# Seven block products in place of eight in all six halves of three feed-forwards

## Chip, cores and metric

The kernel runs on one core of a Trainium2 chip. The metric is the device time of one execution in microseconds, as the median of three runs.

## What is computed

A small diffusion transformer in fp32: width 1024, 256 latent and 256 context tokens, first a block of two layers (a gated linear attention mixer, then a state-space mixer), then a second block of two layers (attention with convolution, then sliding-window and differential attention with a mixture of experts). Each layer takes six modulation vectors from a product of one condition vector with a 1024 x 6144 matrix. The change touches three feed-forwards:

```python
def sq_relu_mlp(h, w1, w2):                  # block 1, layers 0 and 1: w1 1024x4096, w2 4096x1024
    return jnp.square(jax.nn.relu(h @ w1)) @ w2
# block 2, layer 0: w1, w3 1024x2816, w2 2816x1024
# y = (silu(u @ w1) * (u @ w3)) @ w2
# after each: hl = layer_norm(ALPHA * hl + gate * y), or in block 2 hl + gate * y and rms norm ahead of the next mixer
# modulation: m = split(silu(c) @ ada_w[i] + ada_b[i], 6)
```

Layer 0 of block 1 and layer 0 of block 2 work on 512 tokens, layer 1 of block 1 on the 256 latent ones. (The context of the second block is another input, loaded into hT after layer 1's hidden part.)

## The kernel before, in words

Everything is feature major: hT (the residual stream) and uT (the modulated input) hold 8 tiles of 128 features by 512 tokens. A list of stages is built near L2699; each engine runs its own part of each stage in order (`run`, L2736). A stage that isn't `joined` starts with a barrier among TensorE, ScalarE and VectorE (`stage`, L2747): each drains, counts, and waits for the other two. GpSimd runs only stages that are `pooled`.

**Banks.** TensorE's products go round six of the eight PSUM banks (`Banks`, L118). `empty` waits for the bank's last reader, `full` for the product, `freed` for its reader. **Weights.** SyncE streams blocks of up to 2 MB into four slots in a fixed order (`Weights`, L151; L2806); a slot is loaded again when the last product that used it is done.

**Hidden layer, squared ReLU** (`HiddenRelu2`, L932). Eight blocks of 512 columns. Each of 32 hidden tiles is eight 128x128 products with all T tokens (`feature_major`, L821, matmul at L828); the first four tiles run k by k as uT's tiles arrive (`first_features`, L835, L846). ScalarE takes the ReLU from PSUM, VectorE squares it into the arena.

**Down projection** (`Residual`, L858). Eight output tiles, each 32 (or 22) products with all T tokens, one after the other; VectorE adds gate times the product from PSUM to hT (L907), ScalarE squares the new tile (L682), VectorE adds tile and square to two sums (L695, L698). Behind the last tile come the mean and variance (`Norm`, L643), and the next stage's first products wait for the normed and modulated tiles. A barrier stands ahead of this stage.

**Gated hidden layer** (`HiddenSwiglu`, L2179). Its first two tiles are plain; the others go in pairs as seven products (`Seven`, L2078), 128 weight columns by 256 tokens by four k tiles. ScalarE copies the first product, VectorE makes eight additions, GpSimd makes four 512-column sums of weight blocks (L2122 to L2124 and L2130), three of them in a two-deep scratch or in place.

**Guests** (`AdaGuest`, L493). The modulation vectors of later layers are made beside the feed-forwards, 256 columns at a time: ScalarE's queue loads 1 MB into one of two rooms, VectorE adds eight k tiles, each times its condition entry (L576 the first, L573 the other seven, twice that where latent and context are both wanted: a two-sided guest), and TensorE turns the result with two or four short products (L528). A guest has a place among the stage's products; its sums are made at place - 2, the load of the one after the next is issued at place - 1. Before: 24 guests in layer 0's hidden stage (8 two-sided), 24 in its down projection (all two-sided), none in layer 1, 24 in the gated hidden stage (8 two-sided), none in the last down projection.

## Time and profile before

| | us |
|---|---|
| median of 3 runs | 3199.26 (3198.19 to 3200.58) |
| span of the profiled execution | 3197.3 |
| TensorE matmul busy | 3044.7 (95%) |
| VectorE, ScalarE, GpSimd busy | 1338.9, 544.4, 107.2 |
| HBM read | 428.32 MB, 134 GB/s |

The page has a table of busy time by engine, the span in 40 slices, the DMA queues, the chain of work that ended last, and the costliest groups of instructions. The profiled execution is given by its span alone. Matmuls are pipelined, so the mean time of one record is longer than its share of a steady stream: for the price of one, busy time is divided by the count. A 128x128 fp32 weight block against up to 512 columns is two records.

### The profile page before, as it was taken

What the parts mean: (1) busy time and instruction counts of PE and PEld (TensorE: products, weight loads), DVE (VectorE), ACT (ScalarE), POOL (GpSimd) and SP (SyncE); (2) the same over time, 40 slices, a digit from 0 to 9 for tenths busy, and PEclk for the clock granted to TensorE, in tenths of its full rate; (3) what the DMA queues carried; (4) which work ended last, traced back from release to release, by engine and by line L of the source; (5) the groups of instructions that cost most, each with busy time, mean ns of one, the idle gap of its engine ahead of it and who ended that gap; (6) DMA issues with size and microseconds to landing.
All of it is one profiled execution on the core that took longest, in us unless ns stands there. A gap on an engine that the chain in (4) does not pass through costs nothing.

```text
span 3197.3 us, 33171 instructions
## 1 busy us (share of the span) xinstructions
PE 3044.7 (95%) x13248; PEld 2060.0 (64%) x13248; DVE 1338.9 (42%) x3117; ACT 544.4 (17%) x1149; POOL 107.2 (3%) x84
## 2 busy tenths in 40 slices
PE   7999889999999999899999998999999979999999
PEld 2448444444456666788844555888446656999998
DVE  3566465467647777321031327875013342000011
ACT  0215110000033434121021221000012331000000
POOL 0000000000000000000000002343000000000000
PEclk9999999999999999999999999999999988999999
DMA  7550145566322222345521103544222011887785
GB/s 259 171 171 27 53 161 183 156 189 180 115 66 60 79 80 75 109 146 136 154 84 68 53 27 129 174 164 129 76 92 80 27 53 67 289 301 265 267 290 194
DMA packets 395321, 431.58 MB, mean 135 GB/s; under 512 B 15449, under 2 KB 307960, under 8 KB 395034
## 3 DMA queue, kind: packets, MB, share of 16 engines
q1 hardware_dynamic: 294320, 329.77, 31.8%
q10 hardware_dynamic: 100842, 99.62, 9.7%
q8 instruction: 108, 1.77, 0.2%
q14 instruction: 51, 0.42, 0.0%
HBM read 428.32 MB, written 1.05 MB: 134 GB/s over the span
## 4 chain that ended last, share of the span: by engine, by line
PE 90%; DVE 4%; ACT 2%; issue 1%; DMA 0%; DVEq 0%; ACTq 0%
PE bank L828 45%; PE bank L2569 10%; PE bank L2150 7%; PE bank L846 6%; PE bank L2583 4%; PE bank L854 4%; PE bank L528 2%; PE bank L1942 1%; DVE arena L573 1%; PE bank L1935 1%; PE bank L2551 1%; PE bank L2595 1%; PE bank L1539 1%; PE bank L1559 1%; PE bank L1927 1%
## 5 line engine op out<-in xcount | busy, mean ns | idle before, releaser
L828 PE MATMUL bank<-uT,slot 128*128 128x512 f32 (+2 forms) x2208 | 784.9, 512 | 0.0
L828 PE MATMUL bank<-arena,slot 128*128 128x512 f32 (+1 forms) x2016 | 694.0, 506 | 12.9 <-DVEq L2749 10.6
L828 PEld LDWEIGHTS bank<-uT,slot 128*128 128x128 f32 (+1 forms) x2208 | 416.3, 191 | 320.5 <-issue 296.8
L828 PEld LDWEIGHTS bank<-arena,slot 128*128 128x128 f32 x2016 | 386.3, 193 | 299.2 <-issue 275.1
L573 DVE SCALAR_TENSOR_TENSOR arena<-arena,sT 128x256 f32<-128x256 f32 x784 | 365.6, 520 | 7.4
L2569 PE MATMUL bank<-arena,slot 128*128 128x128 f32 x2816 | 316.2, 275 | 3.1 <-issue 2.5
L2569 PEld LDWEIGHTS bank<-arena,slot 128*128 128x128 f32 x2816 | 315.2, 192 | 5.8 <-issue 5.8
L846 PE MATMUL bank<-uT,slot 128*128 128x512 f32 (+1 forms) x448 | 180.4, 568 | 24.7 <-ACT uT L595 12.5
L2654 DVE TENSOR_TENSOR arena<-bank,halves 128x256 f32<-128x256 f32 (+1 forms) x48 | 19.3, 402 | 432.1 <-ACT halves L2615 432.1
L907 DVE SCALAR_TENSOR_TENSOR hT<-bank,mod,hT 128x256 f32<-128x256 f32 (+1 forms) x88 | 36.7, 455 | 370.6 <-PE bank L828 370.6
L846 PEld LDWEIGHTS bank<-uT,slot 128*128 128x128 f32 x448 | 93.1, 209 | 111.7 <-issue 106.4
L2583 PE MATMUL bank<-slot,arena 128*128 128x256 f32 x704 | 153.3, 379 | 1.0 <-DVEq L145 1.0
L2150 PE MATMUL bank<-uT,slot 128*128 128x256 f32 x640 | 148.0, 379 | 0.8 <-DVE arena L2176 0.8
L2583 PEld LDWEIGHTS bank<-slot,arena 128*128 128x128 f32 x704 | 133.7, 190 | 19.3 <-issue 1.2
L2150 PEld LDWEIGHTS bank<-uT,slot 128*128 128x128 f32 x640 | 121.4, 190 | 18.2 <-issue 1.9
L854 PE MATMUL bank<-slot,uT 128*128 128x512 f32 (+2 forms) x352 | 127.3, 515 | 5.7 <-issue 5.7
L682 ACT ACTIVATE halves<-hT 128x512 f32<-128x512 f32 (+1 forms) x49 | 26.4, 538 | 576.5 <-DVE hT L907 531.1
L982 DVE TENSOR_TENSOR arena<-halves 128x512 f32<-128x512 f32 (+1 forms) x64 | 35.7, 558 | 203.8 <-ACT halves L972 203.6
L854 PEld LDWEIGHTS bank<-slot,uT 128*128 128x128 f32 x352 | 62.7, 203 | 66.7 <-issue 66.3
L2122 POOL TENSOR_TENSOR arena<-slot 128x512 f32<-128x512 f32 x20 | 28.2, 1411 | 1868.1 <-DVEq L2749 1868.1
L573 DVE SCALAR_TENSOR_TENSOR rstd<-arena,sT,rstd 128x256 f32<-128x256 f32 x224 | 90.0, 477 | 0.0
L1663 DVE SCALAR_TENSOR_TENSOR arena<-arena,vectors 128x512 f32<-128x512 f32 (+1 forms) x128 | 87.7, 685 | 4.5
(360 smaller groups left out, 2727.0 us busy)
## 6 DMA issues: line engine op xcount, KB each, us to landing
arena<-in_ada_w ACTq DMA_DIRECT2D x88, 1024.0 KB, 5.3
slot<-in_ffn_w SPq DMA_DIRECT2D x42, 2048.0 KB, 9.0
slot<-in_moe_w SPq DMA_DIRECT2D x32, 2048.0 KB, 10.0
slot<-in_moe_w SPq DMA_DIRECT2D x32, 1408.0 KB, 8.9
slot<-in_moe_w SPq DMA_DIRECT2D x16, 1536.0 KB, 9.1
slot<-in_ssd_w_in SPq DMA_DIRECT2D x32, 512.0 KB, 6.8
slot<-in_gla_w_in SPq DMA_DIRECT2D x6, 2048.0 KB, 10.3
slot<-in_ev_w_in SPq DMA_DIRECT2D x6, 2048.0 KB, 7.9
```

The lines of the kernel that those rows point to most:

```text
L528: ins = pe.matmul(ada_cols_bank[:, o:o + 1], acc[:, s, j * P:j * P + P], one[:, 0:1], start=True, stop=True)
L573: ins = dve.scalar_tensor_tensor(out=acc[:, s, :], in0=w[:, k, :], scalar=c, in1=acc[:, s, :], op0=ALU.mult, op1=ALU.add)
L828: ins = pe.matmul(bank[0:m, 0:t1 - t0], w[:, k, c0:c0 + m], x[:, k, t0:t1], start=(k == 0), stop=(k == kt - 1))
L846: ins = pe.matmul(bank[0:m, 0:t], w[:, k, c0:c0 + m], uT[:, k, 0:t], start=(k == 0), stop=(k == KD - 1))
L854: ins = pe.matmul(bank[:, 0:c1 - c0], x[:, k, t * P:t * P + P], w[:, k, c0:c1], start=(k == 0), stop=(k == kt - 1))
L907: return dve.scalar_tensor_tensor(out=h, in0=y, scalar=self.m[:, 8 * self.q + k, s:s + 1], in1=h, op0=ALU.mult, op1=ALU.add)
L982: dve.tensor_tensor(self.hid[:, i, :], r, r, ALU.mult).then_inc(*S("free_a").given())
L1539: ins = pe.matmul(bank[:, h * P:h * P + P], s_dab[k % 2][:, h, :], tri[z], start=True, stop=True)
L1663: ins = dve.scalar_tensor_tensor(out=acc, in0=s_raw[:, j, 0:n, tap:tap + LAT], scalar=vc("conv_w", 32 * tap + f), in1=acc, op0=ALU.mult, o ...
L2150: ins = pe.matmul(bank[:, 0:LAT], a[:, k, :], x[:, k, :], start=(k == 0), stop=(k == self.H - 1))
L2569: ins = pe.matmul(bank[:, o:o + P], w[:, k, (f - c) * P:(f - c) * P + P], m_x[:, k, e * P:e * P + P], start=(k == 0), stop=(k == KD - 1))
L2583: ins = pe.matmul(bank[:, 0:256], hid[:, k, :], w[:, k, :], start=(k == 0), stop=(k == NFE - 1))
```

## The change

The six halves all go by a form of Winograd's scheme with seven products in place of eight: a unit of weights (k tiles in two halves, columns in two halves) times the input (k tiles in two halves, tokens in two halves).

- **Units.** Hidden: 8 k tiles x 512 columns, products of 4 k tiles x 2 column tiles x T/2 tokens. Down: the k tiles are cut in two chunks (16 + 16, or 12 + 10), a unit is one chunk x 256 columns, products of 8 (or 6, 5) k tiles x 1 column tile x T/2 tokens. Order 11, 12, S1, 22, S2, S4, S3; a hidden stage starts with 11 and 12 of its first two units.
- **Weight sums.** GpSimd makes four sums a unit, of a quarter of the unit each (1024 columns, or 768 and 640 in the last down projection), in the slot itself; the second waits for product 11, the third for 12, the fourth for 22.
- **Token differences.** VectorE makes four at the start of each hidden stage and of each chunk of a down projection: the first in place, the others in the arena; a column count of 4 (or 8, 6, 5) x T/2.
- **Evacuation.** ScalarE copies product 11; VectorE makes six operations from PSUM, two of them onto both token halves. The hidden non-linearity is made on whole units by ScalarE. In a down projection the result goes to `halves`, and two (or four) additions put it onto hT at the end of each unit, for each chunk; the norm's squares and sums go along with chunk 1, two tiles a unit.
- **Barriers.** Down is `joined`; signals (hid_done, tiles_done, token_sums, weight_sums, ctx_in) take the barrier's place.
- **Guests** are spread anew: layer 0 hidden 16 (8 two-sided), down 16 (8 two-sided), layer 1 hidden 6 and down 6 (all two-sided), gated hidden 24 (12 two-sided), last down 4 (one-sided). Sums come 4 or 7 products ahead of the guest's place, in two or four parts.
- Six tables of constants are no longer resident, but loaded at the start of OddProject.

```diff
-        class HiddenRelu2(Stage):
+        class Seven:
+            ORDER = ("11", "12", "S1", "22", "S2", "S4", "S3")
+            TOKENS = {"S1": 1, "22": 2, "S3": 1}
...
+            def product(self, pe, bank, w, name, fresh, streamed=None):
+                if name in ("S1", "S2", "S4", "S3"):
+                    pe.wait_ge(*S("weight_sums").taken("pe"))
+                if fresh and name in self.TOKENS:
+                    pe.wait_ge(*S("token_sums").taken("pe", self.TOKENS[name]))
...
+                a = {"11": a11, "12": a12, "S1": a21, "22": a22, "S2": a11, "S4": a12, "S3": a22}[name]
+                x, n, us = self.right[name], self.n, range(a.shape[2] // P)
+                for u in us:
+                    for k in range(self.h):
+                        if streamed and u == 0:
+                            streamed()
+                        ins = pe.matmul(bank[:, u * n:u * n + n], a[:, k, u * P:u * P + P], x[:, k, :], start=(k == 0),
+                                        stop=(k == self.h - 1))
+                ins.then_inc(full_sem, 1)
...
+            def pool(pool, B, w, at):
+                made = S("weight_sums")
+                a11, a12, a21, a22 = Seven.blocks(w)
+                pool.tensor_tensor(a21, a21, a22, ALU.add).then_inc(*made.given())
+                B.full(pool, at("11"))
+                pool.wait_ge(made.sem, made.made)
+                pool.tensor_tensor(a11, a21, a11, ALU.subtract).then_inc(*made.given())
+                B.full(pool, at("12"))
+                pool.wait_ge(made.sem, made.made)
+                pool.tensor_tensor(a12, a12, a11, ALU.subtract).then_inc(*made.given())
+                B.full(pool, at("22"))
+                pool.tensor_tensor(a22, a22, a11, ALU.subtract).then_inc(*made.given())
...
+        class Down(Stage):
+            joined = True
+            pooled = True
+            NU = KD // 2
...
+                cut = 2 * -(-kt // 4)
+                self.chunks = [(0, cut), (cut, kt)]
...
+            def act(self, act, B, ch):
+                if self.guest:
+                    B.full(act, -1)
+                    self.guest.begin(act)
+                self.norm.act_begin(act)
+                for i, (c, u, name) in enumerate(self.order):
+                    if name == "11":
+                        if c + u:
+                            act.wait_ge(S("tiles_done").sem, self.before + c * self.NU + u)
+                        if c and u:
+                            self.norm.act_tile(act, B, 2 * u - 2)
+                            self.norm.act_tile(act, B, 2 * u - 1)
+                        Seven.act(act, B, Tiles(self.out), i)
...
+            def dve(self, dve, B, ch):
+                dve.wait_ge(*self.src.made(self.chunks[0][1]))
+                self.sevens[0].token_sum(dve, 1)
+                B.full(dve, -1)
+                for step in (2, 4, 3):
+                    self.sevens[0].token_sum(dve, step)
+                if self.src.guest:
+                    self.src.guest.dve(dve, ch)
...
+                    if name == "S3":
+                        B.freed(dve, self.index[c, u, "12"])
+                        B.freed(dve, self.index[c, u, "S4"])
+                        B.freed(dve, i)
+                        for j in range(2):
+                            f = 2 * u + j
+                            ins = self.add(dve, j, f, 0, slice(0, LAT))
+                            if self.T == TOK:
+                                ins = self.add(dve, j, f, 1, slice(LAT, TOK))
+                        ins.then_inc(*S("tiles_done").given())
+                    if self.guest:
+                        self.guest.sums(dve, ch, i)
...
-        hid = HiddenRelu2(I["ffn_w1"][0], TOK, AdaGuest(0, 1, all_six, spread, (0, 1)))
-        stages += [hid, Residual(I["ffn_w2"][0], hid.hid, 32, M[0], 5, TOK, False,
-                                 AdaGuest(1, 0, all_six, spread, all_six), Norm(8, M[1], 0, TOK, True))]
+        hid = HiddenRelu2(I["ffn_w1"][0], TOK, AdaGuest(ada01[0:4], spread(8, 52, 16), hidden_guest, 4, 2))
+        stages += [hid, Down(I["ffn_w2"][0], hid, M[0], 5, Norm(8, M[1], 0, TOK, True),
+                             AdaGuest(ada01[4:6] + ada10[0:2], spread(5, 50, 16), down_guest, 4, 2))]
...
+        hid = HiddenRelu2(I["ffn_w1"][1], LAT, AdaGuest(ada10[2:5], spread(14, 52, 6), late_guest, 7, 4, stop=6), ctx=True)
+        stages += [hid, Down(I["ffn_w2"][1], hid, M[1], 5, Norm(24, M[2], 0, LAT, False, True),
+                             AdaGuest(ada10[2:5], spread(8, 48, 6), late_guest, 7, 4, skip=6))]
...
+                           AdaGuest(ada10[5:6] + ada11[0:5], spread(8, 78, 24), late_guest, 4, 2))
+        stages += [hid, Down(I["ffn_w2_2"][0], hid, M[2], 5, Norm(None, M[3], 0, TOK, False),
+                             AdaGuest(ada11[5:6], spread(8, 48, 4), down_guest, 4, 2))]
```

## Rows read from the trace of the kernel before

**Rows 1.** The page's table: busy time, share of span, instructions by engine.
```profile
PE 3044.7 (95%) x13248; PEld 2060.0 (64%) x13248; DVE 1338.9 (42%) x3117; ACT 544.4 (17%) x1149; POOL 107.2 (3%) x84
```
**Rows 2.** Busy time by stretch (length, engines, granted clock, DMA share, GB/s): feed-forward halves.
```profile
393.26:644.13 250.87, 240.95 (x640) 114.74 (x640) 137.67 (x306) 28.46 (x46) 0.00 (x0) 0.96 0.50 159
647.56:892.20 244.64, 244.64 (x706) 120.08 (x707) 162.34 (x414) 4.41 (x7) 0.00 (x0) 0.99 0.53 155
892.20:900.12 7.92, 3.16 (x8) 1.16 (x7) 5.84 (x11) 2.86 (x5) 0.00 (x0) 0.95 0.25 66
1371.20:1484.89 113.69, 113.69 (x514) 99.58 (x515) 16.75 (x42) 19.99 (x46) 0.00 (x0) 0.97 0.47 144
1488.55:1599.30 110.75, 110.75 (x513) 97.52 (x514) 11.46 (x26) 5.47 (x15) 0.00 (x0) 1.00 0.51 145
1931.25:2227.80 296.55, 289.21 (x1312) 242.03 (x1312) 221.59 (x424) 25.53 (x41) 103.21 (x77) 0.98 0.45 146
2231.84:2385.87 154.03, 154.03 (x353) 68.16 (x354) 10.29 (x20) 4.41 (x7) 0.00 (x0) 0.98 0.30 85
```
**Rows 3.** Groups by form (busy us, mean ns, then idle before): matmuls by columns.
```profile
L828 PE MATMUL bank<-arena,slot 128*128 128x512 f32 x1120 | 496.6, 603 | 10.6 <-DVEq L2749 8.3 <-DVE arena L1321 2.3
...
L2569 PE MATMUL bank<-arena,slot 128*128 128x128 f32 x2816 | 316.2, 275 | 3.1 <-issue 2.5 <-DMA slot<-in_moe_w 0.5
```
**Rows 4.** The chain that ended last, in order of time (start, length, piece).
```profile
454.77 6.97 PE bank L828 x16
462.53 6.97 PE bank L828 x16
...
499.99 6.97 PE bank L828 x16
507.30 6.97 PE bank L828 x16
...
2068.27 12.20 PE bank L2150 x56
```
**Rows 5.** Timeline (start, length, engine, line; idle before in brackets), first hidden stage.
```profile
427.98 1.66 PE L528 MATMUL bank<-const,arena 128*128 128x1 f32 x8 [4.91 <-DVE arena L573]
...
434.65 1.87 PE L528 MATMUL bank<-const,arena 128*128 128x1 f32 x8 [5.00 <-DVE arena L573]
...
436.38 8.98 PE L828 MATMUL bank<-uT,slot 128*128 128x512 f32 x14
```
**Rows 6.** Timeline: first products of the three down projections.
```profile
647.56 12.63 PE L828 MATMUL bank<-arena,slot 128*128 128x512 f32 x22 [3.43 <-DVEq L2749]
...
1488.55 11.68 PE L828 MATMUL bank<-arena,slot 128*128 128x256 f32 x53 [1.64 <-DVEq L2749]
...
2231.84 4.60 PE L828 MATMUL bank<-arena,slot 128*128 128x512 f32 x5 [3.98 <-DVEq L2749]
```
**Rows 7.** Timeline, gated hidden stage: guest additions without and beside GpSimd's sums.
```profile
1985.77 3.25 DVE L573 SCALAR_TENSOR_TENSOR arena<-arena,sT 128x256 f32<-128x256 f32 x8
...
1993.16 7.27 DVE L573 SCALAR_TENSOR_TENSOR arena<-arena,sT 128x256 f32<-128x256 f32 x8
1993.36 1.41 POOL L2130 TENSOR_TENSOR slot<-slot,arena 128x512 f32<-128x512 f32 x1 [8.52 <-PE bank L2150]
...
1997.64 1.32 POOL L2124 TENSOR_TENSOR arena<-slot 128x512 f32<-128x512 f32 x1
...
2000.49 1.86 PE L528 MATMUL bank<-const,arena 128*128 128x1 f32 x8 [6.52 <-DVE arena L573]
```
**Rows 8.** Groups by form: a weight sum, a VectorE product, a residual addition.
```profile
L907 DVE SCALAR_TENSOR_TENSOR hT<-bank,mod,hT 128x256 f32<-128x256 f32 x72 | 32.5, 480 | 330.2 <-PE bank L828 330.2
...
L2123 POOL TENSOR_TENSOR slot<-slot 128x512 f32<-128x512 f32 x20 | 26.5, 1323 | 1.6
...
L2288 DVE TENSOR_TENSOR arena<-arena,halves 128x1024 f32<-128x1024 f32 x10 | 13.9, 1387 | 0.8
```
**Rows 9.** Groups by form within the gated hidden stage: all guest additions.
```profile
L573 DVE SCALAR_TENSOR_TENSOR arena<-arena,sT 128x256 f32<-128x256 f32 x224 | 131.3, 620 | 3.4
```

More of the change, by code:

```diff
@@ L522, in pe @@
                     return
+                if n == 0 and self.order:
+                    pe.wait_ge(S("guest_read").sem, self.order)
                 acc = self.room[1][n % 2]
@@ L887, in act @@
                 for k in range(KD):
-                    if self.guest:
-                        self.guest.loads(act, range(4 * k, 4 * k + 4))
                     if self.norm:
@@ L901, in dve @@
                 for k in range(KD):
-                    if self.guest:
-                        self.guest.sums(dve, ch, range(4 * k, 4 * k + 4))
                     bank = B.full(dve, k)
```

628 lines of the change are left out of this document (339 added, 289 removed).

## Prediction

> **What bounds the kernel now.** I read the page's table of busy time first: TensorE is busy 95% of the span and GpSimd 3% [rows 1]. So a microsecond of TensorE work is worth nearly a microsecond wherever it stands, and the question is what the fewer products wake up. Next a table by stretch, one line for each of the six feed-forward halves [rows 2]: H0 and D0 (hidden layer and down projection, 512 tokens), H1 and D1 (256 tokens), HS and D2 (gated hidden layer, 22-tile down projection, 512 tokens). The reader is to see that TensorE is busy in all of each stretch but some 10 us in H0 and 7 us in HS, that VectorE has half or more of H0, D0 and HS, and little in H1 and D1, which have no guest. Then the prices by shape [rows 3]: each fp32 product counts as two records, so a 128x128 block against 512 columns costs 2 x 0.443 us. Then the chain [rows 4]: a group of seven against 256 columns is 56 records in 12.20 us, 0.218 each; against 128 columns the experts' 2816 records take 316.2 us, 0.1123 each. So 256 and 128 columns cost the same per column within 4%: the narrow products of the 256-token halves aren't bound by weight loads.
>
> **1. TensorE's own work.** A unit of H0, H1 or HS (8 x 512 weights) is seven products of two tiles by four blocks: 7 x 8 x 2 = 112 records. A unit of D0 or D1 (a 16 x 256 block) has 7 x 8 x 2 = 112 too.
> H0: 8 units x 112 x 0.218 = 195.2 us. Guests cost TensorE 0.79 us with two sides (pitch 7.76 against 6.97) and 0.34 with one (7.31) [rows 4]; it now has 8 of each: 9.0. Before, the first hidden tiles took four products for each tile of uT that arrived; now two narrow ones. A tile takes VectorE two operations of 512 columns and one of 256, about 0.6 + 0.6 + 0.4 us by the nearest rows [rows 8], and TensorE has done its share of it in 0.44 x 2, so it starves: first four products end at about 18.9 us instead of 14.0, +4.9. Sum 209.1 against 250.9 [rows 2]: **-41.8**. That takes in that the guest at place 2 made TensorE wait 4.91 and 5.00 us, after which 14 records took 8.98 us instead of 6.1 [rows 5]; now the first guest is at place 8 of 56.
> D0: 195.2 + 9.0 = 204.3 against 244.6: **-40.3**.
> H1: 896 x 0.1123 = 100.6, six two-sided guests 4.7, slow start 2.6 (I take the same as its start now costs): 107.9 against 113.7: **-5.8**. D1: 105.3 against 110.8: **-5.4**. A quarter of the gain per column is lost to the narrow width and half the rest to guests that move in.
> HS: ten full units and two of half: 1232 x 0.218 = 268.5, guests 12 x 0.79 + 12 x 0.34 = 13.6, start 2.6: 284.7 against 296.6: **-11.9** (it had seven products in all but two tiles; its waits of 6.5 and 0.8 us go too). D2: 4 x 7 x 11 x 2 = 616 records, 134.2, guests 1.4: 135.6 against 154.0: **-18.4**.
> Sum -123.6 us. If every price were the widest row's, only the last digit moves; what can eat it stands in the next parts.
>
> **2. Barriers.** Between a hidden layer and its down projection TensorE stood 3.43 us (D0), 3.98 us (D2) and 1.64 behind the context's transposes (D1) [rows 6]: -9.0. In their place TensorE's fourth product (the one with factor a22) waits for VectorE: last half's evacuation, then token differences 1, 2 and 4, each 2048 columns in D0 (about 2.5 us, twice the 1.39 of a 1024-column operation [rows 8]), 1024 in D1. VectorE is done near 10.5 us after the hidden layer's last product, plus one GpSimd sum that holds it; TensorE is there at 10.5. I put 3.3 + 2 + 3 = +8.3 us. Price from both sides: 0 if no sum falls in, 15 if each difference meets one.
>
> **3. Tails.** A Down's last product must be added (1024 columns), then four residual additions of 0.45 us [rows 8], then two squares and additions of the norm that lay beside TensorE's last tile before, and the mean's four matmul pairs start only then. Before, the 7.9 us behind D0 [rows 2] held only the last tile's two additions. I add 5 (D0), 2.7 (D1), 3.5 (D2, no mean) = +11.2. From both sides: 6 and 20.
> So far -113.1 us.
>
> **4. GpSimd's sums.** A full unit needs four in-place sums of 1024 columns. No row shows one on GpSimd. The nearest is 512 columns: 1.32 us [rows 8]. Bounds: 1.32 (no growth) and 2.65 (proportional); I take 2.45, since VectorE's price grows a little less than in proportion. The Trainium skill's GPSIMD Engine Reference (3.1 Elementwise) gives 4497 ns for 2048 fp32 elements, which with its dispatch share makes an estimate of 2.3 to 2.4 us: it would change no term. Four sums are about 10 us in a unit of 24.4 us (512 tokens) and in one of 12.6 (256 tokens). The in-place order allows it: after product 11, sums 2, 3 and 4 must be there before S3 starts, 9 us later at 256 tokens; they take 7.6. Cover is there while a sum is under about 2.9 us in H1 and D1 and 5.5 elsewhere.
>
> **5. What the sums do to VectorE.** This is the term that decides. In HS eight guest additions (two SBUF inputs) take 3.25 us without GpSimd and 7.27 us beside four of its sums, and TensorE then waits 6.52 us [rows 7]: a sum that meets them costs VectorE its length less one addition, 1.0 us. Over all of HS the 224 additions take 131.3 us instead of 224 x 0.406 = 91 [rows 9]: 40 us for 77 sums, 0.52 of a hit each, and with the first operation of each guest, which that row doesn't hold, I take 0.65; where VectorE is behind all the time, 0.85. Evacuations read one input from PSUM, and I count them as free. With sums of 2.45 us the price is about 2.1 us, and there are 176 sums in the five halves with many guests: up to 370 us on VectorE. What of it reaches TensorE depends on VectorE's slack there. The Trainium skill's SBUF — State Buffer (Who interferes with whom) says the shared pair is an exclusive lock held for the whole instruction, by a VectorE instruction with two SBUF inputs or by a GpSimd one. By that rule the trace agrees: the 7.27 us row; without the lock the sum would end at parts 1 to 3.
> Per unit, VectorE against TensorE, at a share of 0.65 to 0.85 hits per sum. H0: evacuation 4 x 0.65 + 2 x 1.3 = 5.2, two-sided guests 2.4 x 6.3 (sixteen operations at 0.4) = 15.1, hits 5.5 to 7.1: 25.8 to 27.4 against 26.3 us: +2. HS the same with the gate's product: +3. D0: chunk 1 adds residuals 2.1 and norm 3.2 to 14.7 of guests and 5.2: 30.7 to 32.3 against 26.2, over 3.3 units, with a lag of 8 us brought from the token differences at the end of chunk 0, less what six banks cover (about 14 us): +14. H1: evacuation 3.1, guests 5.5, hits 5.5 to 7.1: 14.1 to 15.7 against 13.3 over six units: +8. D1: 9.5 (chunk 0) and 11.5 (chunk 1) plus hits, 15.0 to 18.6 against 13.3, and 8 us late at its start: +22. D2: +1. Sum **+50 us**, from 6 (banks absorb all but D1's late start) to 119 (below).
>
> **6. Edits at nothing.** Guests' DMA is the same 88 MB spread over more stages, weights come in rows twice as long in the down projections, and the DMA share in these stretches is 0.30 to 0.53 [rows 2]; late constants load behind OddProject's first products; ScalarE has 4 to 28 us of each stretch. If a load were late it would show as TensorE waiting for a slot, some us each.
>
> **Sum.** -123.6 - 9.0 + 8.3 + 11.2 + 50 = -63 us. Against the profiled execution's span of 3197.3 us this is 3134; the median of the runs, 3199.3, is 2.0 above the span, so **3136 us**. A measurement tells about 0.2%, 6.4 us, from no change.
>
> **Rivals.**
> A, the banks absorb the blocking. Six banks let VectorE fall some five products behind, 17 us at 512 tokens, and the guests are asked for four to seven places after their sums. For it: HS already has this blocking and TensorE lost only 7.3 us to it. Against: the sums are twice as long and five halves have them, and D1 has half the time per product. Part 5 is then 6 to 20: 3092 to 3106. Chance 0.22.
> B, every sum stops VectorE for its length (slower). VectorE's lists with all hits at 2.1 us: H0 197 against TensorE's 209 (nothing), D0 238 against 204 (+34), H1 132 against 108 (+24), D1 158 against 105 (+53), HS 293 against 285 (+8): +119, all in stages where VectorE can't keep step, 3205 us, slower by 6. It decides from a share of 1 at 2.1 us a sum, and each 0.1 us more on a sum adds some 12 us. For it: around 1993 us all four sums hit [rows 7]. Against: over HS as a whole the share was 0.52 to 0.65 [rows 9], since VectorE idles between products. Chance 0.13 for ending slower.
> C, the change does less than it says: in H1 and D1 GpSimd is the bound. If a sum takes 3.2 us with what VectorE holds back, a unit lasts 13.5 to 14 us and both halves gain nothing, with part 5 elsewhere: about 3165. For it: one sum waited, but by the rows a sum delayed by an addition grows little. Chance 0.12, inside the range.
> Forecast 0.53 (3107 to 3180).
>
> **Chances and range.** Faster by over 0.2% takes forecast, A and most of C: 0.79. Same: the edge between C and B, 0.08. Slower 0.13. The range 3092 to 3203 leaves out part of B and of A's lower end.
>
> **What would show it.** Right: H0 near 211, D0 near 220, H1 near 116, D1 near 127, HS near 288, D2 near 137 us; GpSimd rows of 128x1024 at 2.4 to 2.6 us, some 200 of them; guest additions with a maximum near 2.6 us instead of 1.48; D1's list of waits headed by TensorE waiting for VectorE. Part 1 is wrong if a seven-group's records at 128 columns run above 0.115 us; part 4 if sums take over 2.9 us; part 5 is too high if D1 is under 112 us, too low if H0 or HS grow past 300 together with waits on guest additions. The clock: waits of 5 us were followed by a stretch at half pace [rows 5], so if part 5 comes in waits of that length, each costs 2 to 3 us on top.

## The result and the profile after

The changed kernel takes 3221.4 us (median; 3217.4 to 3225.9) where the kernel before takes 3199.1 in runs beside it: a ratio of 1.0068, 95% interval 1.0055 to 1.0082. It is **slower by 0.7%**. I had forecast 3136 us with a range up to 3203, so the sign and the range were both wrong.

The page of the changed kernel, its table of busy time (us, share of the span of 3224.1 us, instructions), answers to [rows 1]:

```profile
PE 3004.8 (93%) x15096; PEld 2316.6 (72%) x15096; DVE 1752.1 (54%) x3291; ACT 570.8 (18%) x1143; POOL 486.3 (15%) x212
```

TensorE's busy time fell by only 40 us [rows 1], and its idle time grew from 153 to 219 us. VectorE has 413 us more of busy time. The busy time by stretch of the changed kernel answers to [rows 2], with the same columns (from the half's first product to the next half's; length, then PE, PEld, DVE, ACT, POOL busy, granted clock, DMA share, GB/s). H0, D0, D0's tail, H1, D1, then HS and D2:

```profile
393.15:607.64 214.49, 211.20 (x993) 183.62 (x994) 175.56 (x263) 40.59 (x37) 78.13 (x32) 0.97 0.44 147
607.64:829.10 221.46, 210.61 (x993) 183.82 (x991) 195.32 (x295) 9.90 (x16) 77.04 (x31) 0.98 0.43 137
829.10:844.28 15.18, 6.33 (x10) 2.41 (x9) 8.88 (x16) 3.38 (x6) 0.00 (x0) 0.69 0.13 35
1310.63:1462.16 151.53, 125.92 (x945) 124.20 (x945) 121.35 (x158) 25.02 (x37) 77.79 (x32) 0.85 0.45 150
1464.19:1629.20 165.01, 128.79 (x945) 127.51 (x944) 134.97 (x188) 7.76 (x23) 77.70 (x31) 0.81 0.42 140
...
1965.35:2266.70 301.35, 293.40 (x1385) 256.46 (x1386) 259.41 (x384) 23.90 (x27) 113.82 (x48) 0.97 0.45 150
2266.70:2403.90 137.20, 134.54 (x624) 118.11 (x623) 83.94 (x131) 6.18 (x14) 54.62 (x31) 0.99 0.36 119
```

Of the four halves of 512 tokens three are faster and HS is 5 us slower; H0, D0 and D2 are within 4 us of the forecast, and HS, at 301, is past the 300 us that I had named as a sign of part 5 being too low. H1 and D1, the two halves of 256 tokens, went from 113.7 and 110.8 us to 151.5 and 165.0. There TensorE is idle for 17 and 22% of the time, and runs at a granted clock of 0.85 and 0.81, where it had 0.97 and 1.00 [rows 2].

To leave no time between the stretches out, I compare three regions from here on, each from its hidden half's first product to the first product of the stage behind its down projection: layer 0 (H0, D0), layer 1 (H1, D1) and the swiglu layer (HS, D2). The same view of the kernel before, then of the changed kernel, those three regions in order:

```profile
393.26:900.12 506.86, 488.75 (x1352) 236.02 (x1353) 308.17 (x741) 36.33 (x59) 0.00 (x0) 0.97 0.51 156
1371.20:1615.10 243.90, 235.25 (x1067) 203.07 (x1067) 40.05 (x100) 36.48 (x84) 0.00 (x0) 0.98 0.48 145
1931.25:2391.65 460.40, 445.26 (x1668) 310.54 (x1669) 237.51 (x461) 32.48 (x52) 103.21 (x77) 0.98 0.40 128
```
```profile
393.15:844.28 451.13, 428.15 (x1993) 369.85 (x1993) 379.76 (x574) 53.86 (x59) 155.17 (x63) 0.97 0.43 138
1310.63:1647.99 337.36, 266.65 (x1930) 259.05 (x1931) 268.57 (x377) 44.80 (x84) 155.50 (x63) 0.83 0.43 143
1965.35:2415.01 449.66, 432.02 (x2013) 375.71 (x2013) 347.83 (x523) 33.15 (x46) 168.44 (x79) 0.97 0.42 142
```

-55.7, +93.5 and -10.7 us: together +27.0, the whole difference of the two spans (+26.8). What TensorE waited for in layer 1 of the changed kernel (engine, line, waited for: us in total, times, longest):

```profile
PE bank L549 <- DVE arena L595: 57.8, 12, 7.6
```

L549 is the readout of a guest, L595 its additions: every one of layer 1's 12 guests came late, by 4.8 us on the mean. No wait of TensorE in the changed kernel is put down to GpSimd. The timeline of D1 shows why (start, length, engine, line; what it waited for in brackets):

```profile
1483.95 1.66 DVE L595 SCALAR_TENSOR_TENSOR arena<-arena,sT 128x256 f32<-128x256 f32 x4
...
1485.73 5.84 DVE L595 SCALAR_TENSOR_TENSOR arena<-arena,sT 128x256 f32<-128x256 f32 x4
1485.98 2.43 POOL L1036 TENSOR_TENSOR slot<-slot 128x1024 f32<-128x1024 f32 x1 [3.35 <-PE bank L1024]
1488.56 2.34 POOL L1039 TENSOR_TENSOR slot<-slot 128x1024 f32<-128x1024 f32 x1
...
1493.64 1.84 PE L549 MATMUL bank<-const,arena 128*128 128x1 f32 x8 [5.95 <-DVE arena L595]
...
1495.33 5.04 PE L1024 MATMUL bank<-arena,slot 128*128 128x128 f32 x22
...
1499.13 0.29 DVE L1060 TENSOR_TENSOR halves<-halves,bank 128x128 f32<-128x128 f32 x1 [3.20 <-PE bank L1024]
```

Four additions take 1.66 us when GpSimd is idle and 5.84 us beside two weight sums, and TensorE then stands for 5.95 us. Behind the wait 22 records take 5.04 us, 0.229 each, twice the 0.1123 of [rows 3], and VectorE in its turn stands 3.20 us for the product. The groups by form in D1, VectorE (us busy, mean ns), give the average. L595, L1004 (a token difference) and L1309 (a residual addition) read two operands from SBUF, L598 (a guest's first operation) one, and L1066 (an evacuation) one from SBUF and one from a bank:

```profile
L595 DVE SCALAR_TENSOR_TENSOR arena<-arena,sT 128x256 f32<-128x256 f32 x84 | 66.0, 846 | 0.1
L1004 DVE TENSOR_TENSOR arena<-arena 128x1024 f32<-128x1024 f32 x8 | 15.6, 1950 | 0.3
L1309 DVE SCALAR_TENSOR_TENSOR hT<-halves,mod,hT 128x256 f32<-128x256 f32 x14 | 14.1, 1048 | 0.8
L598 DVE TENSOR_SCALAR arena<-arena,sT 128x256 f32<-128x256 f32 x12 | 9.6, 845 | 0.0
...
L1066 DVE TENSOR_TENSOR halves<-halves,bank 128x256 f32<-128x256 f32 x8 | 3.3, 417 | 4.4 <-PE bank L1024 3.9
```

The weight sums themselves cost close to what I took, 2.45 us; one of the four groups of 52, whose means go from 2282 to 2428 ns with the shorter sums of 512 to 768 columns among them (by form, the 42 of 1024 columns in each group take 2443 to 2557):

```profile
L1033 POOL TENSOR_TENSOR slot<-slot 128x1024 f32<-128x1024 f32 (+3 forms) x52 | 119.9, 2306 | 964.7 <-DMA slot<-in_ffn_w 688.4
```

### The profile page after: what moved, and what is told of

Same layout as the page of the kernel before. It is cut to its first block, busy times and chain, and to the rows that moved or that the text cites. A ratio compares the mean times of both kernels' runs of the same rounds, so it can differ in the third digit from the quotient of the medians.

```text
span 3224.1 us, 37525 instructions
## 1 busy us (share of the span) xinstructions
PE 3004.8 (93%) x15096; PEld 2316.6 (72%) x15096; DVE 1752.1 (54%) x3291; ACT 570.8 (18%) x1143; POOL 486.3 (15%) x212
## 4 chain that ended last, share of the span: by engine, by line
PE 76%; DVE 17%; issue 3%; ACT 2%; DMA 0%; DVEq 0%; ACTq 0%
PE bank L856 20%; PE bank L1024 19%; PE bank L2722 10%; DVE arena L595 6%; PE bank L2736 5%; PE bank L880 4%; PE bank L872 3%; DVE rstd L595 3%; PE bank L549 2%; DVE arena L1004 1%; PE bank L2305 1%; PE bank L2298 1%; DVE arena L598 1%; PE bank L2704 1%; PE bank L2748 1%
## 5 line engine op out<-in xcount | busy, mean ns | idle before, releaser
L1024 PE MATMUL bank<-arena,slot 128*128 128x256 f32 (+1 forms) x3704 | 714.4, 355 | 8.8 <-DVE arena L1004 8.8
L1024 PEld LDWEIGHTS bank<-arena,slot 128*128 128x128 f32 x3704 | 630.1, 201 | 72.7 <-issue 10.1
L856 PE MATMUL bank<-uT,slot 128*128 128x512 f32 (+2 forms) x1312 | 485.8, 525 | 0.0
L856 PEld LDWEIGHTS bank<-uT,slot 128*128 128x128 f32 (+1 forms) x1312 | 245.4, 189 | 210.5 <-issue 199.0
L1024 PE MATMUL bank<-uT,slot 128*128 128x256 f32 (+1 forms) x1728 | 356.5, 366 | 11.6 <-ACT uT L617 11.5
L1024 PEld LDWEIGHTS bank<-uT,slot 128*128 128x128 f32 x1728 | 304.1, 202 | 50.3 <-issue 12.6
L2722 PEld LDWEIGHTS bank<-arena,slot 128*128 128x128 f32 x2816 | 315.2, 192 | 5.8 <-issue 5.8
L595 DVE SCALAR_TENSOR_TENSOR arena<-arena,sT 128x256 f32<-128x256 f32 x420 | 303.5, 773 | 2.6
L1033 POOL TENSOR_TENSOR slot<-slot 128x1024 f32<-128x1024 f32 (+3 forms) x52 | 119.9, 2306 | 964.7 <-DMA slot<-in_ffn_w 688.4
L1036 POOL TENSOR_TENSOR slot<-slot 128x1024 f32<-128x1024 f32 (+3 forms) x52 | 126.3, 2428 | 650.7 <-PE bank L1024 650.3
L856 PE MATMUL bank<-arena,slot 128*128 128x256 f32 (+1 forms) x640 | 199.4, 475 | 3.8 <-DVE arena L1684 2.3
L595 DVE SCALAR_TENSOR_TENSOR rstd<-arena,sT,rstd 128x256 f32<-128x256 f32 x392 | 193.3, 557 | 1.8
L856 PEld LDWEIGHTS bank<-arena,slot 128*128 128x128 f32 x640 | 124.2, 194 | 77.8 <-issue 67.1
L1041 POOL TENSOR_TENSOR slot<-slot 128x1024 f32<-128x1024 f32 (+3 forms) x52 | 118.6, 2282 | 252.4 <-PE bank L1024 252.4
L1039 POOL TENSOR_TENSOR slot<-slot 128x1024 f32<-128x1024 f32 (+3 forms) x52 | 123.4, 2374 | 45.1 <-PE bank L1024 42.0
L595 DVE SCALAR_TENSOR_TENSOR rstd<-uT,sT,rstd 128x256 f32<-128x256 f32 x196 | 126.3, 683 | 2.6
L872 PE MATMUL bank<-uT,slot 128*128 128x512 f32 (+1 forms) x256 | 102.2, 563 | 13.7 <-DVE uT L622 7.6
```

The lines of the kernel that those rows point to most:

```text
L595: ins = dve.scalar_tensor_tensor(out=acc[:, s, :], in0=w[:, k, :], scalar=c, in1=acc[:, s, :], op0=ALU.mult, op1=ALU.add)
L856: ins = pe.matmul(bank[0:m, 0:t1 - t0], w[:, k, c0:c0 + m], x[:, k, t0:t1], start=(k == 0), stop=(k == kt - 1))
L872: ins = pe.matmul(bank[0:m, 0:t], w[:, k, c0:c0 + m], uT[:, k, 0:t], start=(k == 0), stop=(k == KD - 1))
L1024: ins = pe.matmul(bank[:, u * n:u * n + n], a[:, k, u * P:u * P + P], x[:, k, :], start=(k == 0), stop=(k == self.h - 1))
L1033: pool.tensor_tensor(a21, a21, a22, ALU.add).then_inc(*made.given())
L1036: pool.tensor_tensor(a11, a21, a11, ALU.subtract).then_inc(*made.given())
```

## The experiments

My theory after the result: GpSimd's weight sums hold up VectorE's operations with two SBUF operands; in layer 1 this makes guests late, TensorE waits for them, and its clock falls behind the waits. Rivals: GpSimd itself is the bound in layer 1 (rival C of the prediction); the narrow seven-product form is simply slow there; VectorE has too much work, blocked or not; the guests' sums come in too large a burst. The first three kernels take one partner of the collision away each.

**e1: layer 1 without its guests.** Left out: the 12 guests that layer 1 hosts (their adaptive columns are set to 0.5). All sums stay.

```
-  hid = HiddenRelu2(I["ffn_w1"][1], LAT, AdaGuest(ada10[2:5], spread(14, 52, 6), late_guest, 7, 4, stop=6), ctx=True)
+  hid = HiddenRelu2(I["ffn_w1"][1], LAT, ctx=True)
   (and the same for the down projection's guest)
```

> Layer 1's twelve guests are left out (the modulation columns they would make are set to 0.5), all else as in the changed kernel. In the changed kernel the hidden half of layer 1 (H1) takes 151.5 us and its down half (D1) 165.0. Theory L (GpSimd's sums hold guest additions, the guests' bursts outlast TensorE's look-ahead, TensorE waits, and its clock falls after each wait): H1 108 us, D1 106 to 112, granted clock near 1.00 in both, the whole 95 to 105 us shorter, 3116 to 3126. Rival C (the guests are simply too many for units of 12.6 us, sums or no sums) expects the same here. Rival N (128-column products run slow in this place, waits or not): only the waits of 26 and 32 us go, H1 and D1 stay at 122 to 130 each with a clock under 0.9, the whole 3165.

**e2: layer 1 without its weight sums**, guests kept. Left out: the four GpSimd sums of each unit of layer 1; TensorE takes the loaded weights as they are. **e3** leaves them out in all three layers.

```
-  if name in ("S1", "S2", "S4", "S3"):
+  if self.summed and name in ("S1", "S2", "S4", "S3"):
       pe.wait_ge(*S("weight_sums").taken("pe"))
...
-  for q, n in enumerate(self.blocks):
+  for q, n in enumerate(self.blocks if self.seven.summed else ()):
```

> GpSimd's weight sums are left out in layer 1's two halves, with TensorE's waits for them (the products run on unsummed blocks); the twelve guests stay. Theory L: the guest additions fall from 1.0 us to 0.41 each, TensorE's waits for them from 58 us to under 10, H1 109 to 116, D1 108 to 118, the whole 3125 to 3140. Rival C: VectorE has 6.3 us of work per guest in any case, so waits of 30 us or more stay and H1 and D1 are 130 or more each, 3170. Rival N: 122 to 130 each.

> GpSimd's weight sums are left out in all six halves, with TensorE's waits for them. Theory L: what e2 gives and 10 to 20 us in the 512-token halves, mostly in the gated hidden one (301 to about 289), 3105 to 3125. Rival C: the 512-token halves don't change, and the whole stays at 3165 or more. If the sum of parts 1 to 3 of the prediction was right, this run is near 3086 to 3100 plus what guests cost alone.

These three and e7 ran once each. e1 took 3112.1 us and e2 3121.4, both 4 us under what the theory had expected, against 3198.4 before and 3221.4 changed. e3 as a whole took 3622.9: the experts' products run twice there (5632 records in place of 2816), since the numbers and with them the routing are not the true ones, so that only its stretches can be read. Layer 1's region in e1, then e3's three regions, the second of which stands for e2 too (236.99 us there):

```profile
1311.44:1542.72 231.28, 218.52 (x1834) 212.77 (x1835) 108.81 (x185) 44.61 (x84) 153.24 (x63) 0.96 0.46 154
```
```profile
394.83:822.83 428.00, 418.17 (x1992) 365.48 (x1993) 278.96 (x574) 53.95 (x59) 0.00 (x0) 0.99 0.45 146
1291.36:1528.34 236.98, 227.21 (x1930) 221.14 (x1931) 151.66 (x377) 44.79 (x84) 0.00 (x0) 0.97 0.61 203
1844.39:2275.32 430.93, 423.89 (x2013) 371.35 (x2013) 266.93 (x523) 33.24 (x46) 0.00 (x0) 0.98 0.45 148
```

Neither partner alone makes the loss: 231 us with the sums and no guests, 237 with the guests and no sums, 337 with both. GpSimd isn't the bound in layer 1 (rival C falls: e1 has all its sums), and the narrow products aren't slow. e3 gives the price of the sums' interference in each region: 451.1 - 428.0 = 23, 337.4 - 237.0 = 100, 449.7 - 430.9 = 19, together **142 us**. By kind these are 77 us of waits for guests (10.9, 57.8 and 7.9), 9 of waits for token differences (2.2, 4.0 and 2.7), and 58 of longer PE busy time for the same records (10.0, 39.4 and 8.1); e3 keeps 2 us of the waits for guests and none of those for token differences. In e2 no operation of VectorE is held, which gives the unblocked means:

```profile
L595 DVE SCALAR_TENSOR_TENSOR arena<-arena,sT 128x256 f32<-128x256 f32 x168 | 70.3, 481 | 0.1
...
L598 DVE TENSOR_SCALAR arena<-arena,sT 128x256 f32<-128x256 f32 x24 | 7.3, 348 | 0.0
L1310 DVE SCALAR_TENSOR_TENSOR hT<-halves,mod,hT 128x256 f32<-128x256 f32 x16 | 7.0, 482 | 0.9
```

(A mean of 481 ns goes with a pitch of 0.41 us, since one operation's end overlaps the next one's start.) Without the 142 us the change would bring 506.9 + 243.9 + 460.4 - 428.0 - 237.0 - 430.9 = 115 us.

**e7: does the clock follow the waits?** 20 products on constants are put ahead of each wait for a guest in layer 1, so that TensorE works where it stood.

```
   acc = self.room[1][n % 2]
+  if self.filler:
+      for _ in range(20):
+          pe.matmul(ada_rows_bank[:, 0:P], one, one, start=True, stop=True)
   pe.wait_ge(guest_summed, self.summed(n))
```

> In layer 1 TensorE makes 20 extra products (40 records of 128 columns, 4.5 us) of constants into an unused bank ahead of each guest's wait; nothing is left out. It tests what the lower clock comes from. If it comes from standing still: the 896 product records of H1 and D1, 121.6 and 119.5 us busy in the changed kernel against 100.6 at full pace, come down to 101 to 108, the granted clock to 0.95 or more, and the added 54 us cost little or win: H1 130 to 145, D1 140 to 158, the whole 3195 to 3220. Rival N: the records stay near 120 and the filler is added where it isn't covered by a wait, 3221 or more.

It took 3205.2 us, 16 less than the changed kernel, although TensorE got 480 records more. Layer 1 and the products in it, first in e7:

```profile
1312.29:1633.81 321.52, 293.73 (x2411) 286.15 (x2411) 269.24 (x377) 44.75 (x84) 156.03 (x63) 0.94 0.45 150
...
L1028 PE MATMUL bank<-arena,slot 128*128 128x128 f32 x1280 | 156.5, 285 | 4.0 <-DVE arena L1008 4.0
L1028 PE MATMUL bank<-uT,slot 128*128 128x128 f32 x512 | 65.3, 287 | 3.3 <-ACT uT L621 3.3
```

and the products in the changed kernel, with a piece of its timeline:

```profile
L1024 PE MATMUL bank<-arena,slot 128*128 128x128 f32 x1280 | 170.5, 301 | 4.0 <-DVE arena L1004 4.0
L1024 PE MATMUL bank<-uT,slot 128*128 128x128 f32 x512 | 70.7, 302 | 3.3 <-ACT uT L617 3.3
...
1346.54 1.83 PE L549 MATMUL bank<-const,arena 128*128 128x1 f32 x8 [5.67 <-DVE arena L595]
...
1348.24 6.40 PE L1024 MATMUL bank<-uT,slot 128*128 128x128 f32 x32
```

The same 1792 records took 241.2 us in the changed kernel, 221.8 with the filler and 211.8 in e2 (granted clock of the region 0.83, 0.94 and 0.97); 32 of them behind a wait of 5.67 us took 6.40 us at a granted clock of 0.58, where 32 at the full clock take 32 x 0.1123 = 3.6. So the wait is followed by a stretch at the lower of TensorE's two levels, 1.2 GHz in place of 2.4, and keeping the engine at work avoids two thirds of it. That is the second part of layer 1's loss: against e2, PE's busy time in layer 1 is 266.65 - 227.22 = 39.4 us longer for the same records, and its waits for guests 57.8 us: together 97 of the 100.

**e5: the sums of a guest less in a burst.** Layer 1's guests spread their sixteen operations over eight products, starting nine ahead, in place of four and seven (`late_guest, 7, 4` becomes `late_guest, 9, 8`, in both halves).

> Layer 1's guest sums are spread over eight products in place of four, from nine places ahead in place of seven; nothing else. It tells a burst from a lasting overload. If TensorE waits because sixteen additions come in four events (burst): the waits of 26 and 32 us in H1 and D1 fall by half or more, H1 125 to 135, D1 135 to 150, the whole 3175 to 3195. If VectorE is short of time over the whole stage: no change or a few us.

3221.1 us, ratio to before 1.0070 (1.0053 to 1.0086): nothing gained. Layer 1 of e5:

```profile
1315.64:1652.03 336.39, 264.07 (x1930) 255.70 (x1931) 269.00 (x377) 44.81 (x84) 154.47 (x63) 0.86 0.43 143
```

All 12 guests are late as before, 57.7 us of waits. The burst's shape isn't it. VectorE's busy time in the region is 269.0, more than the 237 us in which TensorE could be through: this is a lasting overload, made by the blocking, since the same 377 instructions take 151.7 us in e2.

**e4: layer 1 back to eight products**, with a barrier between the halves, and without sums; it keeps its 12 guests, with their sums two places ahead. **e6** moves 16 more guests there, 8 each from D0 and from HS, so that H1 has 12 and D1 16.

```
-  hid = HiddenRelu2(I["ffn_w1"][1], LAT, AdaGuest(ada10[2:5], spread(14, 52, 6), late_guest, 7, 4, stop=6), ctx=True)
+  hid = EightRelu2(I["ffn_w1"][1], LAT, AdaGuest(ada10[2:5], spread(4, 28, 6), late_guest, 2, 1, stop=6), ctx=True)
...
e6 alone:
-  AdaGuest(ada01[4:6] + ada10[0:2], spread(5, 50, 16), down_guest, 4, 2)
+  AdaGuest(ada01[4:6], spread(8, 48, 8), down_guest, 4, 2)
-  AdaGuest(ada10[5:6] + ada11[0:5], spread(8, 78, 24), late_guest, 4, 2)
+  AdaGuest(ada11[1:5], spread(8, 78, 16), late_guest, 4, 2)
```

> Layer 1 goes back to eight products and the barrier ahead of its down projection; it keeps its twelve guests, at places 4 to 28 and 4 to 27 of 32, sums two places ahead; all else is the changed kernel. Theory L: no sums run there, the guests cost VectorE 6.3 us each out of 18 to 20 between them, TensorE waits for none: H1 113.7 + 4.7 = 118 us, D1 110.8 + 4.7 = 115.5, the gap 2 longer, its tail 3 shorter: 83 us less than the changed kernel, 3138. Rival C: waits for guests stay, 3170 or more.

> As e4, and guests moved into layer 1's eight-product halves, where GpSimd is silent: layer 0's down projection keeps 8 one-sided ones, H1 has 12 two-sided, D1 16 (12 or more two-sided), the gated hidden stage 16 (4 two-sided). Theory L: on top of e4, D0 from 221 to about 206, the gated stage from 301 to about 287, H1 and D1 up by the guests' own matmuls (5 and 8 us), 3115 to 3125. If VectorE runs short in D1 (about 110 us of 120) a wait or two comes back there and it is 3125 to 3140. Rival C: no better than e4.

e4 took 3156.7 us, ratio 0.9868 (0.9851 to 0.9884): the seven-product form of layer 1 had cost 65 us, and the rest of the change is worth 1.3%. I had expected 3138, 83 us less than the changed kernel: I had put 9.4 us for the 12 guests beside eight products, and layer 1 is 21.6 us longer than before the change (265.5 against 243.9). e6 took 3153.6, ratio 0.9855 (0.9839 to 0.9872), which can't be told from e4. Layer 1 of e4, then of e6:

```profile
1315.79:1581.31 265.52, 252.27 (x1162) 216.92 (x1163) 113.06 (x293) 36.42 (x84) 0.00 (x0) 0.96 0.59 180
```
```profile
1295.33:1588.26 292.93, 267.87 (x1291) 231.13 (x1291) 210.17 (x553) 36.43 (x84) 0.00 (x0) 0.96 0.72 221
```

Against the changed kernel e6 won 17 and 12 us in layer 0 and the swiglu layer (433.8 and 437.5 us), and paid them back in layer 1: 27 us over e4, with 16 guests more and waits for guests of 14.7 us in place of 3.3. I had expected 13 us more there, for the guests' own products, and 3115 to 3125 in all. Moving the colliding work was no remedy.

**e8: the same instructions, but the running sum in PSUM.** If it is the second SBUF operand that waits, it need not be in SBUF. The bank `ada_rows_bank` isn't used by then. **e9** is the same edit in the kernel before.

```
+  part_sum = ada_rows_bank[:, :].rearrange("p (s c) -> p s c", s=2) if self.order else acc
...
-  ins = dve.scalar_tensor_tensor(out=acc[:, s, :], in0=w[:, k, :], scalar=c, in1=acc[:, s, :],
+  out = (acc if k == KD - 1 else part_sum)[:, s, :]
+  ins = dve.scalar_tensor_tensor(out=out, in0=w[:, k, :], scalar=c, in1=part_sum[:, s, :],
                                  op0=ALU.mult, op1=ALU.add)
   else:
-      ins = dve.tensor_scalar(acc[:, s, :], w[:, 0, :], c, None, ALU.mult)
+      ins = dve.tensor_scalar(part_sum[:, s, :], w[:, 0, :], c, None, ALU.mult)
```

> The changed kernel with all its weight sums, guests, places and lags, and one thing different: in all guests but those of the first layer's GLA projection, the running sum of a guest (the output of the additions k = 0 to 6) lies in a PSUM bank that the feed-forwards don't use, so an addition reads one operand from SBUF and one from PSUM; only the last of the eight writes the finished sum to SBUF. The same instructions on the same numbers. Theory 'two SBUF operands' (a VectorE operation with two SBUF operands waits for the GpSimd sum in flight, one with a PSUM operand doesn't: in the changed kernel the combinations L1058 to L1069, which read a bank, took 0.42 us in layer 1 while L595 took 1.04): the additions fall to 0.41 to 0.50 us, the waits of TensorE for guests vanish, the regions come to about 432 (layer 0), 240 (layer 1) and 433 us (HS and D2), the whole to 3080 to 3105 us. Theory 'any VectorE operation beside GpSimd': additions stay near 1 us in layer 1, the whole stays at 3215 to 3225. Theory 'too much work on VectorE' (the 16 additions of a guest are too much for it, blocked or not): 3190 to 3225 although the additions are short.

> The kernel before, with the same edit of the guests' running sum (PSUM in place of SBUF, but not in the GLA projection). Before, only one half has GpSimd sums beside guests (HS), where the waits for guests were 6.5 us and blocked additions took 7.3 us in place of 3.3 per eight. 'Two SBUF operands': 5 to 12 us less, 3187 to 3194. If a PSUM operand itself made the additions cheaper or the clock higher (and so explained the gain of the run beside this one): more than 20 us less. If it does nothing: 3199.

e8 took **3116.4 us, ratio 0.9742** (0.9725 to 0.9758): 105 us less than the changed kernel, from one operand; I had expected 3080 to 3105. e9 took 3191.6, ratio 0.9977 (0.9967 to 0.9986): 7.8 us less, with the wait of 6.52 us for the one late guest beside sums [rows 7] gone, and no more. The edit by itself is no gain, only where sums run beside guests. The three regions of e8:

```profile
394.84:828.51 433.67, 421.49 (x1993) 366.88 (x1993) 301.69 (x574) 53.97 (x59) 150.46 (x63) 0.98 0.45 144
1296.27:1559.11 262.84, 235.91 (x1931) 229.17 (x1931) 183.49 (x377) 44.69 (x84) 152.64 (x63) 0.94 0.55 183
1875.16:2310.31 435.15, 425.44 (x2013) 372.30 (x2013) 286.81 (x523) 33.25 (x46) 161.84 (x79) 0.99 0.44 146
```

Layer 0 and the swiglu layer came where I expected them (432 and 433); layer 1 came to 263 in place of 240, with three guests still late (3.2, 7.0 and 3.4 us). The timeline of e8 around the worst of them:

```profile
1474.68 2.35 POOL L1044 TENSOR_TENSOR slot<-slot 128x1024 f32<-128x1024 f32 x1
1474.97 3.15 DVE L1009 TENSOR_TENSOR arena<-arena 128x1024 f32<-128x1024 f32 x1
1477.55 2.77 POOL L1046 TENSOR_TENSOR slot<-slot 128x1024 f32<-128x1024 f32 x1 [0.51 <-PE bank L1029]
1478.04 5.04 DVE L1314 SCALAR_TENSOR_TENSOR hT<-halves,mod,hT 128x256 f32<-128x256 f32 x2
...
1483.00 2.44 DVE L600 SCALAR_TENSOR_TENSOR bank<-arena,sT,bank 128x256 f32<-128x256 f32 x6
...
1486.27 1.87 PE L549 MATMUL bank<-const,arena 128*128 128x1 f32 x8 [7.01 <-DVE arena L600]
```

The additions (L600) keep their 0.41 us apiece, but a token difference takes 3.15 us and two residual additions, which still read two operands from SBUF, 5.04 in place of 0.9; the guest's last additions are queued behind them.

**e10: those guests out of the way.** e8, with the down projection's guests of layer 1 at other places and with more lead.

```
-  AdaGuest(ada10[2:5], spread(8, 48, 6), late_guest, 7, 4, skip=6)
+  AdaGuest(ada10[2:5], spread(14, 52, 6), late_guest, 9, 4, skip=6)
```

> The kernel of e8_psum with the guests of layer 1's down projection at places 14 to 52 in place of 8 to 48 and their sums starting nine products ahead in place of seven. In e8_psum layer 1 kept three waits for guests (3.2, 7.0, 3.4 us), all in the down projection; the longest stood where the sums of the fourth guest shared VectorE with the token differences L1009 (3.15 us each beside GpSimd) and two residual additions (2.5 us each). Theory 'what is left in layer 1 is these operations with two SBUF operands colliding with a due guest': the guest waits fall below 4 us in all and with the clock that follows them layer 1 comes from 263 to 250 to 255 us, the whole to 3104 to 3110 us. If the remaining 263 us are GpSimd or the weights' arrival and not the guests, nothing changes: 3113 to 3119.

**3094.0 us, ratio 0.9670** (0.9657 to 0.9684), the fastest kernel of the study: 3.3% under the kernel before, 127 us under the changed one. Its layer 1, and the largest of what TensorE waited for there from the start of D1 on:

```profile
1294.38:1534.68 240.30, 226.30 (x1931) 220.97 (x1931) 184.16 (x377) 44.69 (x84) 151.27 (x63) 0.98 0.61 200
```
```profile
PE bank L1029 <- DVE arena L1009: 4.0, 1, 4.0
```

No guest is late any more, and the region lost 22.5 us for 13.6 us of waits: 12.9 of it is idle time of PE and 9.6 its busy time, 235.9 against 226.3 us for the same 1931 records. I had expected 250 to 255 us and had counted too little for the clock. More lead had done nothing in e5, where the additions were held; it helps, with the later places, once VectorE can keep up. Which of the two did it, e10 doesn't tell.

**e11: which operand waits?** e8's placing, but the running sum moves to and fro between SBUF and PSUM, so that four forms of the operation meet the same sums.

```
...
+  out, prev = (part_sum, acc) if k % 2 else (acc, part_sum)
+  out = (acc if k == KD - 1 else out)[:, s, :]
+  ins = dve.scalar_tensor_tensor(out=out, in0=w[:, k, :], scalar=c, in1=prev[:, s, :],
                                  op0=ALU.mult, op1=ALU.add)
```

> Places and lags of the changed kernel, as in e8_psum, but a guest's running sum moves to and fro: k = 0 reads SBUF and writes SBUF; k = 1, 3, 5 read two operands from SBUF and write PSUM; k = 2, 4, 6 read one from SBUF and one from PSUM and write SBUF; k = 7 reads two from SBUF and writes SBUF. All forms meet the same GpSimd sums in one execution; in layer 1 the form that waits shows a mean well over its unblocked time of 0.41 to 0.48 us. Theory 'two SBUF inputs': k = 1, 3, 5, 7 at 1.0 to 1.6 us on the mean in layer 1, k = 2, 4, 6 at 0.42 to 0.50. Theory 'a PSUM operand on either side frees it': only k = 7 (and 0) above 0.6. Theory 'an SBUF destination is what waits': k = 0, 2, 4, 6, 7 above 0.6 and 1, 3, 5 not. By the first theory half the additions stay blocked and layer 1 takes 280 to 330 us, the whole 3140 to 3200; by the second about 3125; the whole tells less than the forms do.

The forms in layer 1 of e11 (out<-in, count, us busy, mean ns):

```profile
L601 DVE SCALAR_TENSOR_TENSOR bank<-arena,sT 128x256 f32<-128x256 f32 x72 | 78.3, 1130 | 0.0
L601 DVE SCALAR_TENSOR_TENSOR arena<-arena,sT,bank 128x256 f32<-128x256 f32 x72 | 31.0, 469 | 0.1
L601 DVE SCALAR_TENSOR_TENSOR arena<-arena,sT 128x256 f32<-128x256 f32 x24 | 24.9, 1077 | 0.0
L604 DVE TENSOR_SCALAR arena<-arena,sT 128x256 f32<-128x256 f32 x24 | 17.5, 771 | 0.0
```

Two operands read from SBUF: 1130 and 1077 ns, whether PSUM or SBUF is written. One from SBUF and one from PSUM: 469, no more than the 481 of e2, where nothing is held. That settles the rule for additions: what counts is what is read. The first operation of a guest, which reads one SBUF operand, is held too when it writes SBUF (771 ns against 348) and was not when it wrote PSUM (479 in e8's layer 1, 482 in e9's layer 0, where GpSimd makes no sums). The whole took 3184.3 us, ratio 0.9950 (0.9931 to 0.9970), between e8 and the changed kernel.

## Why the prediction was wrong

**Parts 1 to 3 held, within some 6 us.** They summed to -113.1 us (TensorE's own work, barriers, tails); e3, the change without the sums' interference, brings -115.3 by region. That it is so close is partly luck: part 2 held 8.3 us for TensorE waiting on token differences that a sum delays. The changed kernel does wait 8.9 us for them, but they are gone in e3 and so among the 142; without that term I had -121.4. H0 at 214.5, D0 at 221.5 and D2 at 137.2 stand beside the 211, 220 and 137 I gave. In e10 the 128 records between two guests of H1 took 14.40 us, 0.1125 each, the price of part 1; the 0.135 of the changed kernel (241.2 us for 1792 records), over the 0.115 that I had named as a sign against part 1, is the clock behind the waits. The tail of D0 is 15.2 us in place of 7.9, +7.3 where I said +5, the largest error of the three tails.

**Part 4 was right.** Sums of 1024 columns took 2.44 to 2.56 us on the mean (I took 2.45); e1 shows that GpSimd was no bound in layer 1, so rival C is out.

**Part 5 is the step that failed**: +50 us forecast, with 119 as its upper bound; +142 measured, 133 without the waits of part 2. By region I had given layer 0 16 us, layer 1 30 and the swiglu layer 4; it was 23, 100 and 19. The step has two halves, and they failed unequally.

What the sums cost VectorE I had nearly right. Its busy time is longer than in e3 by 379.76 - 278.96 = 100.8 us in layer 0 (63 sums), 268.57 - 151.66 = 116.9 in layer 1 (63) and 347.83 - 266.93 = 80.9 in the swiglu layer (79): 1.6, 1.9 and 1.0 us a sum, against the 1.4 to 1.8 of my working (a share of 0.65 to 0.85 of 2.1). Layer 1 was a little above and the swiglu layer below. Not counted by name were the token differences, residual additions and norm, which wait just as the guests' additions do; e8 and e10 show them at work.

What of that cost reaches TensorE I had wrong. I set VectorE's work for one unit against TensorE's time for it and let only the excess through: H1 15.7 against 13.3, D1 18.6. That takes a stage where VectorE is behind to run at VectorE's pace, with VectorE busy all the time. It wasn't: it was busy 268.6 of 337.4 us, 80%, and in e5 269.0 of 336.4, 80% again, in e11 251.4 of 313.6, 80%. Each engine waits for the other in turn, as the rows of D1 above show. TensorE stands before a guest's readout until the additions are through; by then VectorE has done all it was given, and must wait for the next product to evacuate (44 of its 69 us of idle time in layer 1); that product comes at half the clock. With VectorE's demand in layer 1 above the 237 us that TensorE needs, 86% of VectorE's extra time arrived at TensorE (100.4 of 116.9); in layer 0 and the swiglu layer, where its demand stayed under TensorE's time, 23% did (23.1 of 100.8, 18.7 of 80.9). My own demand for H1 and D1, eight units of 14.1 to 15.7 and eight of 15.0 to 18.6 us, is 233 to 274 us; over 0.8 that is 291 to 343 us, which holds the 316.5 that the two halves took. The 0.8 is read off these runs afterwards and no run tried the loop by itself; but it is what my sum had no place for.

**The clock** I had named as a caveat, "2 to 3 us on top" for a wait of 5 us, and left out of the sum. It was two fifths of the loss, 58 of 142 us, more by itself than all of part 5: 39.4 us of busy time beside 57.8 of waits for guests in layer 1, 0.68 us for each us waited, 9.6 to 13.6 (0.71) between e8 and e10. For a wait of 5 us that is 3.4, near the caveat's size; [rows 5] had shown it, 8.98 us for 6.1, and it belonged in part 5.

**Rival B** was the right neighbour, a VectorE that can't keep step with D1 and H1 the worst, but it put the deciding point at every sum hitting, and its price at +119 us, 3205 in all; VectorE's own cost a sum was under its 2.1 us everywhere and the time went past 3205 all the same, since waits are dearer than the excess they come from. D0, where it saw +34, lost less: all of layer 0 lost 23. Its sign, slower, had a chance of 0.13 from me. **Rival A**, the banks absorb the blocking, holds in part for the halves of 512 tokens, which lost 42 us where it gave 6 to 20 for all six, and fails for those of 256: a bank lets VectorE fall behind with evacuations, but a guest that is due has no bank in between.

The Trainium skill's SBUF — State Buffer (Who interferes with whom) says that a VectorE instruction with two SBUF inputs contends with a GpSimd one that reads SBUF, and that one with at most one SBUF input outside the two-port modes doesn't. By that rule the traces agree: 469 ns against 1130 and 1077 in e11. A guest's first operation, with one SBUF input and held all the same (771 ns), fits that rule only if it runs in a two-port mode; its faster pace unheld, 348 ns against 479 with PSUM written, points there, but no run settles it. I had read the rule as a price alone and passed over the remedy that follows from it: the running sum could have been in PSUM.

The change as made is thus -115 us of saved work and +142 us of interference, of which e8 takes back 105 by one operand and e10 127 by that and a later placing. What is left, some 15 us in all, is mostly in layer 0 (433.8 against 428.0) and the swiglu layer (435.1 against 430.9); layer 1 is 3.3 us over e3. That it is the token differences, residual additions and norms, the operations with two SBUF operands that remain, fits their lengths (residual additions in e10's D1: 1161 ns on the mean, 482 in e2) but was not tried by itself.

## What to carry to other kernels

Before moving work to GpSimd, list VectorE's operations in the same stretch that read two operands from SBUF, and see whether one of the two can be in PSUM: here that one operand was worth 105 us, and decided between slower and faster. When one engine's extra work has to be turned into time, don't set averages against each other if the two wait for each other in order: take the waits, add what the clock does behind them (here 0.7 us for each us waited), and expect neither engine to be busy all the time. A stage that has half the time per product for the same additions is the one to look at first.

## What the hardware did that I had not expected

- An operand in PSUM costs VectorE nothing here: 469 to 483 ns on the mean for an addition of 256 columns in e8 and e11, 481 with both operands in SBUF and nothing in the way. Beside a GpSimd sum the one is as long as ever, while two residual additions with both operands in SBUF took 5.04 us.
- A multiplication by a scalar with a single SBUF operand (L598) is held by GpSimd's sums too when it writes SBUF, 762 and 845 ns on the mean in H1 and D1 against 348. Writing PSUM it takes 479 beside the sums and 482 without any: the faster pace is gone, and the hold with it.
- Products put in where TensorE would wait shorten the whole: 480 more records in e7 took 16 us off the kernel, by a granted clock of 0.94 in layer 1 in place of 0.83.
